# Adding a visit's expert results to the tokens on chip in the next visit

## What is computed

```python
logits = jnp.dot(t, w_router).astype(jnp.float32)
top_val, top_idx = lax.top_k(logits, TOP_K)            # TOP_K = 2 of N_EXPERTS = 8
top_w = jax.nn.softmax(top_val, axis=-1)
gates = jnp.einsum('tk,tke->te', top_w, one_hot(top_idx, N_EXPERTS))
def expert(args):
    e_w1, e_w3, e_w2, g = args                         # 1024 x 3584, 1024 x 3584, 3584 x 1024
    hid = jax.nn.silu(t @ e_w1) * (t @ e_w3)
    return (hid @ e_w2) * g[:, None]
y = jnp.sum(lax.map(expert, (w1, w3, w2, gates.T)), axis=0)
```

## Time and profile before

| | us |
|---|---|
| median of 3 runs | 1884.84 (1882.88 to 1887.56) |
| profiled execution, its own time | 1884.7 |
| its span | 1883.0 |
| PE busy | 1726.2 (92%) |
| DVE busy | 634.5 (34%) |
| ACT busy | 527.1 (28%) |
| POOL busy | 93.3 (5%) |

### The profile page before, as it was taken

How to read it: one execution, slowest core, us unless ns; L and a number is a source line. 1 busy time by engine, 2 the same in 40 slices (tenths; PEclk the granted TensorE clock), 3 DMA queues, 4 the chain that set the end, 5 groups by cost and what they waited for, 6 DMA issues and landing times.

```text
span 1883.0 us, 37010 instructions
## 1 busy us (share of the span) xinstructions
PE 1726.2 (92%) x16015; PEld 1097.0 (58%) x16015; DVE 634.5 (34%) x1104; ACT 527.1 (28%) x903; POOL 93.3 (5%) x107
## 2 busy tenths in 40 slices
PE   6999998999987989999988999799978989998776
PEld 3776677886666779998875353324423352443223
DVE  3654845236774756556664000000000000000011
ACT  3335824334544654344452000000000000000001
POOL 0120000111210000000001000000000000000000
PEclk9999999999998999999999999999999999999999
DMA  8362024754335735555539999999999999999996
GB/s 328 132 233 80 2 90 158 208 160 91 56 104 193 190 124 190 185 196 184 190 112 363 330 421 421 413 424 413 424 414 424 413 421 421 405 423 408 424 420 253
DMA packets 169900, 510.26 MB, mean 271 GB/s; under 512 B 27673, under 2 KB 54721, under 8 KB 153361
## 3 DMA queue, kind: packets, MB, share of 16 engines
q1 hardware_dynamic: 163824, 491.82, 69.5%
q0 software_dynamic: 4864, 15.54, 2.5%
q10 hardware_dynamic: 1056, 0.57, 0.1%
HBM read 499.47 MB, written 8.41 MB: 270 GB/s over the span
## 4 chain that ended last, share of the span: by engine, by line
PE 67%; DMA 11%; issue 8%; DVE 6%; ACT 5%; SPq 2%; POOL 1%; ACTq 0%; POOLq 0%; DVEq 0%
PE bank L2631 20%; PE bank L2085 10%; PE bank L2086 10%; PE bank L2087 10%; PE bank L2624 8%; DMA ring_t<-in_e_w 5%; DMA ring_h<-in_e_w 2%; SPq L764 2%; DMA ring_w<-in_e_w 2%; ACT w_hi L851 1%; DVE w_lo L1258 1%; PE bank L2107 1%; PE bank L2264 1%; PE bank L2253 1%; DMA raw<-in_e_w 1%
## 5 line engine op out<-in xcount | busy, mean ns | idle before, releaser
L1258 DVE TENSOR_TENSOR w_lo<-raw,w_hi 128x2048 fp32r<-128x2048 f32 x98 | 224.2, 2291 | 202.2 <-ACT w_hi L851 202.2
L2085 PE MATMUL bank<-h_hi,w_hi 128*128 128x256 f32 (+1 forms) x864 | 261.3, 302 | 4.6 <-DVE w_lo L1258 3.2
L2086 PE MATMUL bank<-h_lo,w_hi 128*128 128x256 f32 (+1 forms) x864 | 258.1, 299 | 0.0
L2087 PE MATMUL bank<-h_hi,w_lo 128*128 128x256 f32 (+1 forms) x864 | 258.1, 299 | 0.0
L851 ACT ACTIVATE w_hi<-raw 128x2048 fp32r<-128x2048 f32 x98 | 187.0, 1911 | 165.4 <-PE bank L2087 101.6
L1906 DVE TENSOR_TENSOR act_f<-act_s,bank 128x512 f32<-128x512 f32 (+1 forms) x40 | 22.7, 617 | 529.1 <-PE bank L2631 529.1
L2631 PE MATMUL bank<-ring_w,xe 128*32 128x512 f32 (+1 forms) x1920 | 188.0, 540 | 12.8 <-DMA ring_w<-in_e_w 12.8
L2085 PEld LDWEIGHTS bank<-h_hi,w_hi 128*128 128x128 f32 x864 | 165.3, 191 | 13.6 <-DVE w_lo L1258 5.4
L2086 PEld LDWEIGHTS bank<-h_lo,w_hi 128*128 128x128 f32 x864 | 165.4, 191 | 5.6 <-issue 0.2
L2087 PEld LDWEIGHTS bank<-h_hi,w_lo 128*128 128x128 f32 x864 | 165.3, 191 | 5.1
L2631 PEld LDWEIGHTS bank<-ring_w,xe 128*32 128x32 f32 x1920 | 59.3, 110 | 139.3 <-issue 106.0
(11 more groups left out here) (359 smaller groups left out, 2150.0 us busy)
## 6 DMA issues: line engine op xcount, KB each, us to landing
ring_w<-in_e_w SPq DMA_DIRECT2D x72, 1024.0 KB, 18.9
ring_h<-in_e_w SPq DMA_DIRECT2D x64, 1024.0 KB, 17.9
ring_t<-in_e_w SPq DMA_DIRECT2D x48, 1024.0 KB, 17.4
raw<-in_e_w SPq DMA_DIRECT2D x40, 1024.0 KB, 18.1
ring_w<-in_e_w SPq DMA_DIRECT2D x48, 768.0 KB, 22.0
raw<-in_w SPq DMA_DIRECT2D x33, 1024.0 KB, 5.1
raw<-in_w_qkv SPq DMA_DIRECT2D x24, 1024.0 KB, 5.0
ring_h<-in_e_w SPq DMA_DIRECT2D x32, 768.0 KB, 21.6
```

Of the source, the lines that this page charges most:

```text
L1258: nc.vector.tensor_tensor(w_lo[:, split_slot(m), :], raw_unit(m), w_hi[:, split_slot(m), :].bitcast(F32), ALU.subtract).then_inc(lo_ready, 1)
L2085: nc.tensor.matmul(out_, a_hi, b_hi, start=start, stop=False)
L2086: nc.tensor.matmul(out_, a_hi, b_lo, start=False, stop=False)
L2087: return nc.tensor.matmul(out_, a_lo, b_hi, start=False, stop=stop)
```

## The change

Every visit now adds its results as only the last one did, but in the next visit. In each visit DVE builds `pick_g` from the slot numbers behind its first product, PE turns it at unit 37 (in banks 0 to 2) and ACT copies it to `pick_gt`, ahead of `turn_rows`, which waits for it. In the next visit PE, behind unit 1, waits for `y_ready` and does `combine`: for each of two token halves, each group and each of four row groups one matmul of 32 x 128 by 256 into banks 3, 4, 5 and 7. DVE, at the head of its visit, adds the four banks to `xs`, and PE waits for that ahead of unit 8. The stores to `result_rows`, the tensor itself, its zeros, `places` and the fetch of the rows are gone. The gather of the next tokens asks for 64 or 96 rows as the next visit is wide. The order of ranks changes so that WIDE visits are 0, 2, 3, 4, and visits 0 to 5 are written out one by one with no loop on PE, ACT, DVE and POOL; SP's loop stays. The padding ahead of `ring_t` grows by what the removed tiles held.

```diff
-RANK_AT = [0, 4, 1, 5, 2, 3, 6, 7]
-PAIRED, TWO_WIDE = 4, 6
+RANK_AT = [0, 4, 1, 2, 3, 5, 6, 7]
+FIRST_VISITS = [WIDE, NARROW, WIDE, WIDE, WIDE, NARROW]
...
+COMBINE_BANKS = [3, 4, 5, 7]
...
-    result_rows = nc.dram_tensor("result_rows", [VISITS, SLOTS, D], F32, kind="Internal").ap()
...
-                if last:
-                    act.wait_ge(sem("pick_turned"), 1)
-                    for t in range(groups):
-                        ins = nc.scalar.activation(pick_gt[:, t, :], bank[t][:, 0:TOK], ACT.Copy)
-                    ins.then_inc(sem("pick_gt_ready"), 1)
-                else:
+                act.wait_ge(sem("pick_turned"), v + 1)
+                for t in range(groups):
+                    ins = nc.scalar.activation(pick_gt[:, t, :], bank[t][:, 0:TOK], ACT.Copy)
+                ins.then_inc(sem("pick_gt_ready"), 1)
+                if not last:
...
-                    ins.then_inc(sem("y_taken"), 1)
-
-            with act.Fori(0, PAIRED, 2) as v:
-                visit(v, WIDE, False)
-                visit(v + 1, NARROW, False)
-            with act.Fori(PAIRED, TWO_WIDE) as v:
-                visit(v, WIDE, False)
+                    ins.then_inc(sem("y_ready"), 1)
+
+            for v, groups in enumerate(FIRST_VISITS):
+                visit(v, groups, False)
...
-                if last:
-                    places()
+                if not isinstance(v, int) or v:
+                    dve.wait_ge(sem("y_combined"), v)
+                    for b in range(4):
+                        x = xs[:, 0:TT, b * TOK:(b + 1) * TOK]
+                        y = bank[COMBINE_BANKS[b]][:, 0:TT * TOK].rearrange("p (t n) -> p t n", t=TT)
+                        nc.vector.tensor_tensor(x, x, y, ALU.add).then_inc(sem("y_added"), 1)
                 gated(0)
-                if last:
-                    for t in range(TT):
-                        dst = pick_g[:, t, 0:groups * P].rearrange("p (a b s) -> p a b s", a=groups, b=4)
-                        src = pick[:, t, 0:groups * TILE].rearrange("p (a s) -> p a s", a=groups).unsqueeze(2)
-                        ins = nc.vector.tensor_scalar(dst, src.broadcast_to([P, groups, 4, TILE]), current[:, 4 + t:5 + t], None, ALU.mult)
-                    ins.then_inc(sem("pick_g_ready"), 1)
-                    for t in range(TT):
-                        dve.wait_ge(sem("rows_back"), 32 * (t + 1))
-                        for choice in range(2):
-                            nc.vector.scalar_tensor_tensor(xs[:, t, :], xs[:, TT + choice, :], gates[:, t, 2 + choice:3 + choice], xs[:, t, :],
-                                                           ALU.mult, ALU.add).then_inc(sem("row_added"), 1)
-                            dve.wait_ge(sem("row_added"), 2 * t + choice + 1)
-                else:
+                now = current if not isinstance(v, int) or v else visits[:, 0, :]
+                for t in range(TT):
+                    dst = pick_g[:, t, 0:groups * P].rearrange("p (a b s) -> p a b s", a=groups, b=4)
+                    src = slot_number[:, 0:groups * TILE].rearrange("p (a s) -> p a s", a=groups).unsqueeze(2)
+                    ins = nc.vector.tensor_scalar(dst, src.broadcast_to([P, groups, 4, TILE]), now[:, t:t + 1], now[:, 4 + t:5 + t],
+                                                  ALU.is_equal, ALU.mult)
+                ins.then_inc(sem("pick_g_ready"), 1)
+                if not last:
+                    dve.wait_ge(sem("pick_g_ready"), v + 1)
                     picks(v + 1)
...
-            nc.gpsimd.memset(none[:], 0.0).then_inc(sem("pool_step"), 1)
-            pool.wait_ge(sem("pool_step"), 1)
-            for v in [n for n in range(VISITS) if n >= EXP or RANK_AT[n] >= WIDE_RANKS]:
-                pool.dma_start(result_rows[v].rearrange("p (a n) -> p a n", a=4), none[0:SLOTS, :].unsqueeze(1).broadcast_to([SLOTS, 4, TOK]))\
-                    .then_inc(sem("no_rows_stored"), 16)
-            pool.wait_ge(sem("no_rows_stored"), 16 * (VISITS - WIDE_RANKS))
...
+                rows = groups * TILE
                 pool.wait_ge(sem("slot_token_ready"), v + 1)
                 pool.nop().then_inc(sem("pool_step"), 1)
-                pool.indirect_dma_start(slot_row[0:SLOTS, :], None, token_rows, bass.IndirectOffsetOnAxis(ap=slot_token[0:SLOTS, 0:1], axis=0))\
+                pool.indirect_dma_start(slot_row[0:rows, :], None, token_rows, bass.IndirectOffsetOnAxis(ap=slot_token[0:rows, 0:1], axis=0))\
                     .then_inc(sem("slot_row_landed"), 16)
-                pool.wait_ge(sem("y_taken"), v + 2)
-                pool.nop().then_inc(sem("pool_step"), 1)
-                for b in range(4):
-                    dst = result_rows[bass.ds(v, 1), 0:groups * TILE, b * TOK:(b + 1) * TOK].rearrange("a (t s) n -> s (a t) n", s=TILE)
-                    pool.dma_start(dst, y_row[b * TILE:(b + 1) * TILE, 0:groups, :]).then_inc(sem("result_rows_stored"), 16)
-                pool.wait_ge(sem("result_rows_stored"), v * 64 + 64)
-                pool.nop().then_inc(sem("row_buffer_free"), 1)
...
+            for v in range(len(FIRST_VISITS)):
+                visit(v, (FIRST_VISITS + [NARROW])[v + 1])
...
-            pool.wait_ge(sem("place_ready"), 1)
-            pool.wait_ge(sem("x_gathered"), last_visit * 2)
-            all_rows = result_rows.rearrange("v p d -> (v p) d")
-            for t in range(TT):
-                if t:
-                    pool.wait_ge(sem("row_added"), 2 * t)
-                for choice in range(2):
-                    pool.nop().then_inc(sem("pool_step"), 1)
-                    pool.indirect_dma_start(xs[:, TT + choice, :], None, all_rows,
-                                            bass.IndirectOffsetOnAxis(ap=place_row[:, t, choice:choice + 1], axis=0))\
-                        .then_inc(sem("rows_back"), 16)
...
-                    pe.wait_ge(sem("act_s_ready"), v * 2 + 2)
+                    pe.wait_ge(sem("pick_gt_ready"), v + 1)
...
+                def combine(before):
+                    pe.wait_ge(sem("y_ready"), v)
+                    for tok in range(TT):
+                        for t in range(before):
+                            for b in range(4):
+                                part = slice(b * TILE, (b + 1) * TILE)
+                                ins = nc.tensor.matmul(bank[COMBINE_BANKS[b]][:, tok * TOK:(tok + 1) * TOK],
+                                                       pick_gt[part, t, tok * P:(tok + 1) * P], y_row[part, t, :],
+                                                       start=tok == 0 and t == 0, stop=tok == TT - 1 and t == before - 1)
+                    ins.then_inc(sem("y_combined"), 1)
+
                 for n, (kind, p, c) in enumerate(visit_units):
+                    if n == 2 and (not isinstance(v, int) or v):
+                        combine((FIRST_VISITS + [NARROW])[v - 1] if isinstance(v, int) else NARROW)
+                    if n == CH and (not isinstance(v, int) or v):
+                        pe.wait_ge(sem("y_added"), v * 4)
                     if n == 2 * CH + 3:
                         turn(0)
                     if n == 2 * CH + 5 and not last:
                         next_tokens()
                     if n == 4 * CH + 3:
                         turn(1)
-                    if n == 4 * CH + 5 and last:
+                    if n == 4 * CH + 5:
...
-                            pe.wait_ge(sem("y_taken"), v + 1)
...
-            with pe.Fori(0, PAIRED, 2) as v:
-                visit(v, WIDE, False)
-                visit(v + 1, NARROW, False)
-            with pe.Fori(PAIRED, TWO_WIDE) as v:
-                visit(v, WIDE, False)
+            for v, groups in enumerate(FIRST_VISITS):
+                visit(v, groups, False)
```

More of the change, by code:

```diff
@@ L2649, in visit @@
                                 ins.then_inc(sem("x_combined"), 1)
-            with pe.Fori(0, PAIRED, 2) as v:
-                visit(v, WIDE, False)
-                visit(v + 1, NARROW, False)
-            with pe.Fori(PAIRED, TWO_WIDE) as v:
-                visit(v, WIDE, False)
+            for v, groups in enumerate(FIRST_VISITS):
+                visit(v, groups, False)
             pe.wait_ge(sem("routed"), 1)
             last_visit = pe.value_load(ids[0:1, 15:16], min_val=EXP - 1, max_val=VISITS - 1)
-            with pe.Fori(TWO_WIDE, last_visit) as v:
+            with pe.Fori(len(FIRST_VISITS), last_visit) as v:
                 visit(v, NARROW, False)
```

50 lines of the change are left out of this document (7 added, 43 removed).

## The result

The changed kernel took a median of 1862.88 us (1861.9 to 1865.45, 4 runs) against 1884.12 (1882.88 to 1887.56, 4 runs) for the one before: ratio 0.9889, 95% interval 0.9873 to 0.9905, 21 us. The profiled execution took 1862.72 us, its span is 1860.9. The forecast was 1869.0 with a range of 1862 to 1878. The time lies inside, 0.9 us above the lower end, where rival (a) put it.

The account below looks back on a forecast made before the run. Loads at 420 GB/s were taken as the bound, PE only with the ring full. Zero stores 7.6, clock 1.2 and removed transfers 11.9, less 5 for the ring, gave 15.7 us off 1884.7: 1869.0 us, range 1862 to 1878.

Parts of the forecast that it names:

- rival (a): Expert visits: the ring never binds, and the first part keeps its full clock share; 21.7 us gained, 1863 us; chance 0.22.
- What bounds the kernel: Expert visits: loads at 420 GB/s bound the sum; PE bounds only while the ring of 16 slots is full.
- Zero stores and clock: Stage of qkv0: without the zero stores a delayed load lands sooner, 7.6 us, and the clock behind recovers, 1.2 us.
- The new wait for the slot: Stage of qkv0: the split next waits for PE to free its w_hi slot; PE still idles about 1.1 us.
- The ring: WIDE visits 2 to 4: loads want a lead of 33 us, 28 fit; about 5 us of load time lost.
- (b): Expert visits: the ring binds early, a loss of 13 us; 7.7 us of gain stays, 1877 us; chance 0.16.
- (c): Stage of qkv0: zero stores only double the load, which lands at 569.3, 5.0 us earlier; 1872.8 us; chance 0.07.
- (d): Mid-visit combine: its four matmuls don't run side by side, 4.0 us a group; slower, 1893 us; chance 0.04.
- Edits costed at nothing: Expert visits: loop returns removed, DVE's additions, new waits, ACT's copies and pick_g, each taken as covered, at nothing.

Follow-up runs that it names:

- e1: Changed kernel with only the ten zero stores put back on POOL behind the roots of n2: 1871.03 us, ratio 0.9937.
- e2: Changed kernel with the order of visits of before (WIDE at 0, 2, 4, 5): 1862.96 us, ratio 0.9889.
- e8: Changed kernel with all removed transfers, gathers of 96 rows and the old order put back; combine on chip and straight code stay: 1881.81 us, ratio 0.9989.
- e7: Changed kernel with the combine's matmuls of each visit done four times: 1894.57 us, ratio 1.0052.
- e5: Changed kernel without PE's combine and DVE's additions in visits 1 to 7: 1862.39 us, ratio 0.9885.
- e6: Changed kernel with the combine's matmuls of each visit done twice: 1871.29 us, ratio 0.9933.

## Why the prediction was right, and where it was wrong

**What bounds the kernel: right.** The loads set the expert part. It fell by 11.8 us for 11.9 us of bytes, while PE was busy 12.9 us longer, and the transfers put back cost about their bytes (5.0 for 5.6, 4.1 for 5.0).

**Zero stores and clock: right.** 7.6 + 1.2 = 8.8 us foretold, 8.1 measured (e1). In the two single traces the experts start 10.1 us earlier, so some 2 us of that aren't the stores'. 1.0 us is there before the gap: PE's last group of k ends at 571.6 and at 572.6 in the trace of before, which has a stretch at half clock from 524 us on, ahead of the stores; the one after has none there. It's likely chance of the profiled execution, since e2, whose program differs from the changed one only in the order of visits, has such a stretch again, and starts the experts 1.0 us later. Busy times of before and then of after:

```profile
520.00:530.00 10.00, 7.61 (x42) 5.07 (x41) 5.96 (x14) 4.49 (x11) 0.00 (x0) 0.83 0.32 105
```

```profile
520.00:530.00 10.00, 7.49 (x61) 4.97 (x60) 6.10 (x15) 5.49 (x14) 0.00 (x0) 1.00 0.27 102
```

The new wait for the slot, 1.1 us of idle PE foretold, is 1.38.

**The ring: the step that failed.** "About 5 us of load time is lost with the ring full" was right as far as it goes: 4.7 us were held back, in visit 4, at 357 to 396 GB/s. The step from there to the sum, that load time held back is time lost, was wrong by the whole 5 us, or by 4 to 5 if the 0.4 to 1.0 us between the traces is real. I had taken the sixteen engines for one with a rate of 420 GB/s. They are sixteen, here in two groups of eight of unlike speed, and the last sets the time; the ring stops those ahead. So the forecast's arithmetic held up to 15.7 us and the 4.7 us came back at the end, which makes 20.4 of the 21 us measured. The rest is less than the interval of the ratio (3 us); the 2 us of straight code that I had at nothing (e8) and the 0.7 by which the zero stores were put too high lie within it.

**Rival (a)** gives the measured time, but by another way than its own: the ring did bind. That the time lay in the range is owed to the range taking in (a), not to the sum, which was 6.1 us too high. **(b)** would have needed the loss ahead of visit 4. **(c)** is out: the split started at 565.96 and waited for PE, not for a load at 569.3. Read as equal shares of time, the rule of turns in the Trainium skill ("DMA: Bandwidth & Descriptors", "Queues, rings and completion order") does not give the delay; of turns as such the completion records decide nothing: the delayed load of before had its first part in at 567.0 and its last at 574.3, and the same load without the stores at 559.8 and 560.3. **(d)** was refuted by 2.80 us for three groups; e7 made it real, and it came out at 1894.57 for the 1893 worked out, in part by luck, since the cost of the two NARROW visits was missing from my sum and the repaid 5 us were in it.

**Edits costed at nothing.** DVE's additions with all their waits, and with them the combine: nothing (e5). The order: nothing (e2), against the gain of 4 to 5 us that a ring loss would have given back. This cover is thin: a second combine cost its full length (e6).

## What to carry to other kernels

Where loads never pause, price a removed transfer at its bytes over the rate of that stretch, and look at what else the DMA engines move while a load is under way that an in-order engine waits for: there stores on another queue that nobody waits for cost 8 us. A full ring is not yet a loss; in this kernel it first brought the engines level again, and only behind that was each us of compute a us of time, so judge an order of wide and narrow stages by what the next edit will add, not by today's time. Test a term of the sum by taking its cause away: the dip was where it had been foretold, and still it cost nothing.

## What was not expected of the hardware

- The sixteen DMA engines drift apart in two groups of eight while they never pause, from 1 us at 1040 to 10 to 12 us near 1800, in every trace without a full ring on the way. In the kernel without gathers the distance also grew, to 7.4 us at 1420, so the gathers are not its only cause; what is, stays open.
- Ten stores of 384 KB in rows of 1 KB beside a load of 1 MB made its sixteen parts land over 7.3 us where without the stores they landed within 0.5 us. The load is late by its slowest part.
- The half-clock stretches that stood behind the two loop returns of before (granted clock 0.97 over 1500 to 1600) are gone with the loops, in e8 too. (Not every such stretch needs a return: e2, without these loops, has one of 3.4 us from 1373.5.) The same stretch in the changed kernel:

```profile
1500.00:1600.00 100.00, 100.00 (x1371) 46.99 (x1367) 7.35 (x16) 7.92 (x19) 0.90 (x1) 1.00 1.02 419
```

- A gather of 96 rows pulls the rate of its stretch from 424 to some 404 GB/s (from 1580 to 1600 e2 has 407, and the kernel without gathers 420), and yet 128 rows more cost 1.0 us by the medians, about their bytes. The runs are too few to tell this from twice the bytes.
